# One-hot arrays of an expert-routing stage: one VectorE instruction a token in place of wide ones on VectorE and GpSimd

## The reference

```
q = (x1 @ wq)                          # 8 heads, 2 halves of 128
s = q . subkeys                        # 128 keys for each half
sv, si = top_k(s, 16)                  # for each half
fv, fi = top_k(all 256 pair sums, 16)
i1, i2 = si[half 0][fi // 16], si[half 1][fi % 16]
g = softmax(fv);  e = i1 * 128 + i2    # 128 x 128 experts
y = sum over 8 heads, 16 picks of  g * gelu(u_tab[e] . x1) * v_tab[e]
```

## Time and profile before

| | |
|---|---|
| median of three runs | 4511.48 us |
| profiled execution | 4522.91 us, span 4521.1 us |
| granted TensorE clock, mean | 0.891 |
| busy: TensorE, VectorE, ScalarE, GpSimd | 79%, 56%, 17%, 15% |
| DMA | mean 185 GB/s |

### The profile page before, as it was taken

How to read it: one execution, slowest core, us unless ns; L and a number is a source line. 1 busy time by engine, 2 the same in 40 slices (tenths; PEclk the granted TensorE clock), 3 DMA queues, 4 the chain that set the end, 5 groups by cost and what they waited for, 6 DMA issues and landing times.

```text
span 4521.1 us, 60266 instructions
## 1 busy us (share of the span) xinstructions
PE 3564.3 (79%) x21641; PEld 2009.5 (44%) x21641; DVE 2525.8 (56%) x5218; ACT 759.6 (17%) x1241; POOL 693.6 (15%) x650
## 2 busy tenths in 40 slices
PE   4999646887765656227888898988889888898998
PEld 2555643444665555223334343443434434344354
DVE  3111544442777888835656565565655655556555
ACT  2110222211001111111111111111111111111122
POOL 0000000000002333331221212212122121221101
PEclk8999768998876666559999999999999999999999
DMA  6211333333000222257776777767777777777622
GB/s 174 80 68 59 108 133 143 115 108 132 15 10 5 79 79 74 74 177 295 270 299 255 285 287 282 296 255 284 285 281 293 264 279 269 279 300 268 240 98 97
DMA packets 274890, 835.65 MB, mean 185 GB/s; under 512 B 38088, under 2 KB 143856, under 8 KB 213200
## 3 DMA queue, kind: packets, MB, share of 16 engines
q0 software_dynamic: 64512, 469.79, 27.2%
q1 hardware_dynamic: 210272, 364.48, 23.7%
HBM read 742.12 MB, written 93.39 MB: 185 GB/s over the span
## 4 chain that ended last, share of the span: by engine, by line
PE 28%; DMA 9%; DVE 6%; DVEq 5%; issue 4%; ACT 1%; SPq 1%; POOL 1%; PEld 0%; POOLq 0%; ACTq 0%; PEldq 0%
PE experts_ps L1532 12%; PE experts_ps L1519 8%; PE experts_ps L1505 5%; DMA experts_ut<-in_uT 4%; DMA experts_rows<-in_uv,experts_place 4%; PE experts_ps L1494 3%; DVEq L1660 3%; DVE experts_prod L1657 2%; DVEq L1685 1%; DVE experts_hl L1688 1%; DVE experts_hf L1684 1%; DVEq L1667 1%; DVE experts_hh L1686 1%; ACT experts_act_a L1571 1%; DMA experts_shift<-in_ln_b 1%
## 5 line engine op out<-in xcount | busy, mean ns | idle before, releaser
L1598 POOL DMA_INDIRECT experts_rows<-in_uv,experts_place x448 | 454.1, 1014 | 1810.1 <-PE experts_ps L1505 1684.7
L1519 PE MATMUL experts_ps<-experts_xh,experts_uh 128*128 128x320 f16 x2048 | 622.2, 304 | 77.7 <-DMA experts_eye<-in_c_eye 55.7
L1657 DVE CUSTOM_DVE_ANT_0 experts_prod<-experts_rows,experts_ps 128x1024 f32<-128x1024 f32 x448 | 545.2, 1217 | 148.4 <-DMA experts_rows<-in_uv,experts_place 98.6
L1519 PE MATMUL experts_ps<-experts_xl,experts_uh 128*128 128x320 f16 x2048 | 619.9, 303 | 0.0
L1519 PE MATMUL experts_ps<-experts_xh,experts_ul 128*128 128x320 f16 x2048 | 619.3, 302 | 0.0
L1532 PE MATMUL experts_ps<-experts_vh,experts_hh 128*128 128x512 f16 x1280 | 489.5, 382 | 3.0 <-DVEq L1689 2.8
L1532 PE MATMUL experts_ps<-experts_vl,experts_hh 128*128 128x512 f16 x1280 | 486.8, 380 | 0.0
L1532 PE MATMUL experts_ps<-experts_vh,experts_hl 128*128 128x512 f16 x1280 | 486.2, 380 | 0.0
L1697 DVE SCALAR_TENSOR_TENSOR experts_y<-experts_ps,experts_y 128x512 f32<-128x512 f32 x320 | 221.0, 691 | 451.8 <-PE experts_ps L1532 440.3
L1494 PE MATMUL experts_ps<-experts_xr,experts_pick 32*128 32x512 f16 x896 | 271.9, 383 | 242.3 <-DVE experts_dot L1657 240.6
L1519 PEld LDWEIGHTS experts_ps<-experts_xh,experts_uh 128*128 128x128 f16 x2048 | 202.1, 99 | 274.4 <-issue 182.4
(11 more groups left out here) (252 smaller groups left out, 5145.5 us busy)
## 6 DMA issues: line engine op xcount, KB each, us to landing
experts_ut<-in_uT SPq DMA_DIRECT2D x128, 512.0 KB
experts_vt<-in_uv SPq DMA_DIRECT2D x128, 512.0 KB, 4.9
scratch_g<-route_gbuf SPq DMA_DIRECT2D x5, 8192.0 KB, 30.4
experts_g<-scratch_g SPq DMA_DIRECT2D x128, 320.0 KB, 3.2
scratch_z<-project_z SPq DMA_DIRECT2D x10, 1984.0 KB, 7.1
project_piece<-in_w_in SPq DMA_DIRECT2D x15, 1024.0 KB, 5.7
merge_w_piece<-in_w_merge SPq DMA_DIRECT2D x13, 1024.0 KB, 7.6
mix_za<-scratch_z SPq DMA_DIRECT2D x10, 960.0 KB, 5.6
```

Of the source, the lines that this page charges most:

```text
L1519: mm = pe.matmul(ps[:, p % 2, 0:W], w[:, m % 2, t, :], x[:, t, c * W:(c + 1) * W], start=t == 0 and j == 0, stop=t == KT - 1 and j == 2)
L1598: pool.indirect_dma_start(rows[:, t % RING], None, a.uv.rearrange("r e d -> (r e) d"), bass.IndirectOffsetOnAxis(ap=place[:, t:t + 1], axi ...
L1657: dve.tensor_tensor_reduce(prod[:].rearrange("p (c n) -> p c n", c=2), rows[:, q % RING, 0:D].rearrange("p (c n) -> p c n", c=2), ps[:, 4: ...
```

## The change

Each batch now has three VectorE instructions for each of its eight tokens. A token's index and gate are columns of one element a partition, taken as scalars: `hot_c` is one compare with the column index; `hot_h` and `hot_l` are one compare with the row index, multiplied by the high or low part of the gate. `hot_r` and GpSimd's part with its semaphores are gone. The arrays lie as [token, key], each 128 elements dense; the scalars are f32, so `col` becomes f32 and `high` is an f32 copy of the f16 gate. The loop over batches is written out (16 times) instead of being a loop of the engine with four batches in its body. TensorE's matmuls read the dense arrays; their number and order stay.

```
-        ident, iota, iota16 = s.sb("ident", [P, P]), s.sb("iota", [P, KEYS, QT], F16), s.sb("iota16", [P, TOPK])
+        ident, iota, iota16 = s.sb("ident", [P, P]), s.sb("iota", [P, KEYS], F16), s.sb("iota16", [P, TOPK])
...
-        hot_r, hot_c = s.sb("hot_r", [P, 2, G, KEYS, QT], F16), s.sb("hot_c", [P, 2, G, KEYS, QT], F16)
-        hot_h, hot_l = s.sb("hot_h", [P, 2, G, KEYS, QT], F16), s.sb("hot_l", [P, 2, G, KEYS, QT], F16)
...
+        hot_c, hot_h, hot_l = (s.sb(k, [P, 2, BT, KEYS], F16) for k in ("hot_c", "hot_h", "hot_l"))
...
-                        pe.wait_ge(lows_ready, d * batches + b + 3)
...
-                                pe.matmul(o, hot_c[:, half, q, :, t], hot_h[:, half, q, :, t], start=True, stop=False)
-                                mm = pe.matmul(o, hot_c[:, half, q, :, t], hot_l[:, half, q, :, t], start=False, stop=True)
+                                n = q * 4 + t
+                                pe.matmul(o, hot_c[:, half, n, :], hot_h[:, half, n, :], start=True, stop=False)
+                                mm = pe.matmul(o, hot_c[:, half, n, :], hot_l[:, half, n, :], start=False, stop=True)
...
-                        pool.tensor_tensor(hot_l[:, half], hot_r[:, half], spread(gl[:, bass.ds(b * BT, BT)]), ALU.mult)
-                        pool.drain().then_inc(lows_ready, 1)
...
-                    dve.wait_ge(lows_ready, d * batches + 2)
+                    dve.wait_ge(g_full, d * batches * 2 + 4)
...
-                    dve.tensor_tensor(gl[:], gt[:], gh[:], ALU.subtract)
+                    dve.tensor_copy(high[:], gh[:])
+                    dve.drain()
+                    dve.tensor_tensor(low[:], gt[:], high[:], ALU.subtract)
...
-                    def batch(b, half):
+                    for b in range(batches):
+                        half = b % 2
                         dve.wait_ge(g_full, (d * batches + b) * 2 + 2)
-                        dve.wait_ge(const_loaded, 64)
-                        now = bass.ds(b * BT, BT)
-                        dve.tensor_tensor(hot_r[:, half], numbers, spread(col[:, 0, now]), ALU.is_equal)
-                        dve.drain().then_inc(rows_ready, 1)
-                        dve.tensor_tensor(hot_c[:, half], numbers, spread(col[:, 1, now]), ALU.is_equal)
-                        dve.tensor_tensor(hot_h[:, half], hot_r[:, half], spread(gh[:, now]), ALU.mult)
+                        for n in range(BT):
+                            t = slice(b * BT + n, b * BT + n + 1)
+                            dve.tensor_scalar(hot_c[:, half, n, :], iota[:], col[:, 1, t], None, ALU.is_equal)
+                            dve.tensor_scalar(hot_h[:, half, n, :], iota[:], col[:, 0, t], high[:, t], ALU.is_equal, ALU.mult)
+                            dve.tensor_scalar(hot_l[:, half, n, :], iota[:], col[:, 0, t], low[:, t], ALU.is_equal, ALU.mult)
                         dve.drain().then_inc(hots_ready, 1)
-                    over_batches(dve, batch)
```

More of the change, by code:

```diff
@@ L1022, in route_stage @@
         gsum = s.sb("gsum", [P, PH])
-        col = s.sb("col", [P, 2, P], F16)
-        gt, gh, gl = s.sb("gt", [P, P]), s.sb("gh", [P, P], F16), s.sb("gl", [P, P], F16)
-        hot_r, hot_c = s.sb("hot_r", [P, 2, G, KEYS, QT], F16), s.sb("hot_c", [P, 2, G, KEYS, QT], F16)
-        hot_h, hot_l = s.sb("hot_h", [P, 2, G, KEYS, QT], F16), s.sb("hot_l", [P, 2, G, KEYS, QT], F16)
-        one, scrap = s.sb("one", [P, 1]), s.sb("scrap", [P, 1])
+        col = s.sb("col", [P, 2, P])
+        gt, gh = s.sb("gt", [P, P]), s.sb("gh", [P, P], F16)
+        high, low = s.sb("high", [P, P]), s.sb("low", [P, P])
+        hot_c, hot_h, hot_l = (s.sb(k, [P, 2, BT, KEYS], F16) for k in ("hot_c", "hot_h", "hot_l"))
         place_f = s.sb("place_f", [P, 2, P])
@@ L1038, in route_stage @@
         pickT_full = s.sem("pickT_full")
-        rows_ready, lows_ready = s.sem("rows_ready"), s.sem("lows_ready")
         hots_ready, places_ready, places_stored = s.sem("hots_ready"), s.sem("places_ready"), s.sem("places_stored")
@@ L1057, in over_batches @@
                     body(j * 4 + k, k % 2)
-        def spread(values):
-            return values.rearrange("p (g t) -> p g t", t=QT).unsqueeze(2).broadcast_to([P, G, KEYS, QT])
-        numbers = iota[:].unsqueeze(1).broadcast_to([P, G, KEYS, QT])
         with nc.Block() as block:
@@ L1197, in _ @@
                 over_steps(act, body)
[L1199 to L1207, removed]
-                    def batch(b, half):
-                        pool.wait_ge(rows_ready, d * batches + b + 1)
-                        pool.tensor_tensor(scrap[:], one[:], one[:], ALU.mult)
-                        pool.tensor_tensor(hot_l[:, half], hot_r[:, half], spread(gl[:, bass.ds(b * BT, BT)]), ALU.mult)
-                        pool.drain().then_inc(lows_ready, 1)
-                    over_batches(pool, batch)
-                over_steps(pool, body)
             @block.vector
@@ L1757, in shape_constants @@
         "c_tril": np.triu(np.ones((P, P), np.float32)),
-        "c_iota": np.broadcast_to(np.arange(KEYS, dtype=np.float16)[None, :, None], (P, KEYS, QT)).copy(),
+        "c_iota": np.broadcast_to(np.arange(KEYS, dtype=np.float16), (P, KEYS)).copy(),
         "c_iota16": np.broadcast_to(np.arange(TOPK, dtype=np.float32), (P, TOPK)).copy(),
```

## The result

The changed kernel takes 4581.43 us (median of four runs, 4571.25 to 4584.4) where the kernel before takes 4513.08 beside it: ratio 1.0146, 95% interval 1.0129 to 1.0164. A second series gave 4582.78, ratio 1.0156 (1.0140 to 1.0171). It is 68 us slower; 4580.5 had been forecast.

The account below looks back on a forecast made before the run. VectorE was taken to bound each block of the stage. Four blocks at +13.3 us, the last at +14.7 and 1.5 for copies sum to +69, from the median 4511.5 to 4580.5; range 4500 to 4655.

Parts of the forecast that it names:

- Start to start: New VectorE instructions: the next starts 163 ns after a one-scalar one, 226 after a two-scalar one; 4.92 us per eight tokens.
- four one-scalar instructions in sequence against the pair with constants: Old VectorE trace: four 128x136 f32 instructions start 201 ns apart, two 128x128 without scalars 140, so scalar loads are paid.
- Scalars not hidden, against the rule: VectorE: each scalar's load is paid every time, about 63 ns, though the skill's rule knows no charge for scalars.
- Width: VectorE's new instructions: f16 halves the columns' time as in two-source rows, 33 ns for 128 columns instead of 67.
- The gap between batches: VectorE between batches: the old 0.47 us falls to 0.32, and to 0.25 in the last block.
- Before the batches: VectorE before each block's batches: one copy to f32 and its drain add 0.3 us, 1.5 over five blocks.
- the prediction's signs: What the trace should show, among others batches 5.3 us apart and about 133 us from routing to routing instead of 119.9.
- What lies beside it: Other engines: the third batch's 1.99 us wait for TensorE does not return; dense columns cost nothing, with up to 2 us gain.
- rival (2): VectorE: scalar loads are hidden, instructions 106 ns apart, third batch 4.3 us late for TensorE; -101 us, 4410; chance 0.10.
- (3): VectorE: the second scalar comes free with the first, third batch stalls 1.6 us; -5 us, 4506, no change; chance 0.09.
- The stall behind GpSimd: Old batch: VectorE's high product stands 1.69 us behind GpSimd's low product, ending 0.69 after it; the stall goes entirely.
- point of decision: VectorE's start-to-start distance: faster or slower is decided at 4.18 us a batch, a mean of 170 ns an instruction.

Follow-up runs that it names:

- e1: Changed kernel with constants in place of all per-partition scalars (fixed keys and gates): 4410.1 us, 108 below the kernel before.
- e2: Changed kernel with constant gates, so each of the 24 instructions has one per-partition scalar: 4517.53 us, difference 0 from the kernel before.
- e6: Changed kernel with the compared numbers 0 to 127 in f32 instead of f16: 4641.16 us, 127 above the kernel before.
- e3: Kernel before without GpSimd's low product (hot_l stays zero): 4391.96 us, 126 below the kernel before.
- e4: Kernel before with the low product moved from GpSimd to VectorE as a fourth wide instruction: 4446.55 us, 71 below the kernel before.
- e7: e4 with the next block's score groups spread over the first four batches and VectorE's batches written out: 4395.22 us, ratio 0.9739 to the kernel before.
- e5: Changed kernel with VectorE's loop over the dense blocks written out: 4562.7 us, 48 above the kernel before.
- e8: e7 with VectorE's loop over the dense blocks written out as well: 4382.21 us, ratio 0.9710 to the kernel before.

## Why the prediction was right

It was right in its mechanism, and its terms were of the right size; two small misses of opposite sign, and some luck outside the stage, make the last 1 us of agreement worth little.

- **Start to start.** Forecast 163 and 226 ns, measured 163 and 223. The step that carried it was the reading of four one-scalar instructions in sequence against the pair with constants. e1 and e2 show each load apart: 103, 163, 223.
- **Scalars not hidden, against the rule.** The Trainium skill's figure of some 75 ns an instruction after queue overlap (Vector Engine (DVE) Microarchitecture Reference, section 5.2, Measured stream behaviour) gives 108 with the columns, an estimate. e1 agrees with it, at 103. With scalars the rows decide, 60 more for each, so it does not price this change.
- **Width.** 33 ns for 128 f16 columns, 34 less than in f32: e6 shows 32 between the two.
- **The gap between batches.** Forecast 0.32, and 0.25 in the last block; measured 0.21 and 0.12. With it, and with 223 in place of 226 ns, a block is 82.5 us, not 85.0, and the last one 81.2 (from its first batch at 1942.92 to 2024.07), not 83.9. Four times 10.9 and 11.9 make +55, where +68 had been forecast.
- **Before the batches.** +0.3 a block was forecast. From the copy of the picks to the first batch of the second block it is 1.74 us (1544.93 to 1546.67), where it was 1.81 (1537.56 to 1539.37): the extra copy is there, but a gap of 0.52 before the first batch shrank to 0.15.
- **What was missed.** The unrolled loop's own cost, at the jump back: 3.1 us in place of 0.8, three times, +7.0. I had costed the unrolling only as a gain. From routing to routing it is 133.4 us (1546.67 - 1413.31), as the prediction's signs had it, but by luck: the batches give 10.9 of the growth and the jump 2.3, where the batches alone were to give 13.3.
- **The sum.** From the first batch of the first block to the end of the last it was 548.1 us (1419.50 to 1967.59) and is 610.8 (1413.31 to 2024.07): 55.3 from the blocks, 7.0 from the jumps, 0.4 from the routings and the loop's end, +62.7. What lies before and behind in the stage is 0.8 shorter, and the stage grew by 61.9. The forecast of the stage was 69, 7 too high.
- **The rest.** The medians differ by 68, 6 more than the stage. Outside the stage the one profile of before took 3611 us and the two of the changed kernel 3598 and 3608, less and not more, and the profiles of all kernels spread over 25. These 6 us stay open.
- **What lies beside it.** The wait for TensorE at the third batch is gone, as forecast, and came back where VectorE became faster with the scores left in their place (18.9 us in e1, 7.3 in e2, 21.8 in e3, 17.0 in e4); rivals (2) and (3) had priced it at 4.3 and 1.6 a block, and e1 and e2 show 4.7 and 1.8. The dense columns changed little: matmuls follow each other at 0.107 us (ten steps from 1603.80 to 1604.87 in the changed kernel), 0.118 before, both at a granted clock of 0.50 (1.2 GHz), in the shade of VectorE.
- **The stall behind GpSimd.** Its size was right, 1.69 us forecast and 1.70 in e3. One reading beside it was not: the high product ends 0.55 us after GpSimd's instruction, not 0.69.
- **The rivals.** e1 is rival (2) built: 101 us faster than before was its price, 108 was measured. Its point of decision, a mean of 170 ns an instruction, is bracketed by e2 (163, no change) and the changed kernel (203).

## What to carry to other kernels

A per-partition scalar has a price of its own, also in a row of such instructions: at 128 f16 columns each cost 60 ns, nearly twice as much as the columns themselves (33), so here short instructions with scalars lost to one wide two-source instruction with broadcast operands. When an engine's instruction takes several times as long as its twin, look for what runs beside it: here the stall was GpSimd's instruction, and moving GpSimd's work onto the busier engine made the stage shorter. Before unrolling inside a loop that stays, count what the jump back will cost.

## What the runs showed of the hardware

- VectorE, 128 columns f16, start to start: 103 ns with constants, 163 with one per-partition scalar, 223 with two.
- A wide f16 two-source instruction of VectorE takes 684 ns beside an idle GpSimd and 2382 beside a GpSimd instruction of 2402; it ends 0.55 us after GpSimd's.
- A jump back over a long body idles VectorE for 3.1 to 3.4 us (changed kernel, e7), over the shorter body of before, which has a loop of four batches in it, 0.78; straight code, 0.15 (e5, e8).
- A wait against a register's value between batches costs 0.09 us more than one against a constant (0.21 and 0.12).
